# Strassen's scheme of seven products in the first matmul of both feed-forward parts of an encoder trunk

## What is computed

```python
FF = 2816; D_MODEL = 1024
def swiglu(xn, w_in, w_out):
    gu = xn @ w_in                  # w_in: (1024, 5632), gate columns, then up columns
    g = gu[..., :FF]
    u = gu[..., FF:]
    return (jax.nn.silu(g) * u) @ w_out   # w_out: (2816, 1024)

xn = rmsnorm(h, norm_ffn[i]); h = h + swiglu(xn, ffn_w_in[i], ffn_w_out[i])
```

## Time and profile before

| | |
|---|---|
| runs of the kernel before | 2137.39 us median of 3 (2136.59 to 2147.86) |
| span of the profiled execution | 2135.1 us |
| PE, weight loads | 2074.0 us (97%), 1865.6 us (87%) |
| DVE, ACT, POOL | 840.1, 448.3, 722.5 us (39%, 21%, 34%) |
| matmuls | 11553 |
| DMA | 110.93 MB, mean 52 GB/s |

### The profile page before, as it was taken

The page is one execution under the profiler, slowest core; times in us unless marked ns, Lnnn a source line. Parts: engine busy times, 40 slices in busy tenths (PEclk is TensorE's granted clock), DMA queues, the critical chain, the costliest instruction groups (busy, mean ns, idle before and its releaser), DMA issues.

```text
span 2135.1 us, 30482 instructions
## 1 busy us (share of the span) xinstructions
PE 2074.0 (97%) x11553; PEld 1865.6 (87%) x11553; DVE 840.1 (39%) x1458; ACT 448.3 (21%) x895; POOL 722.5 (34%) x423
## 2 busy tenths in 40 slices
PE   7999999999999999999999999999899999999999
PEld 7787878899999999999978777787788888888887
DVE  6544354543221222124655555556442212221231
ACT  4222322322100010001233333334221100100001
POOL 3221312234443444444411111111244444443443
PEclk9999999999999999999999999999899999999999
DMA  3111111122222222221211111010122222222222
GB/s 115 40 30 30 49 30 40 30 72 60 66 61 59 59 59 60 59 63 53 71 30 30 30 30 29 20 29 20 40 60 59 69 59 66 62 62 67 59 59 89
DMA packets 213393, 110.93 MB, mean 52 GB/s; under 512 B 5283, under 2 KB 212294, under 8 KB 213334
## 3 DMA queue, kind: packets, MB, share of 16 engines
q1 hardware_dynamic: 209264, 108.28, 17.4%
q10 hardware_dynamic: 4070, 1.81, 0.3%
HBM read 106.93 MB, written 3.15 MB: 52 GB/s over the span
## 4 chain that ended last, share of the span: by engine, by line
PE 92%; DVE 4%; issue 2%; ACT 1%; DMA 0%; DVEq 0%; ACTq 0%; SPq 0%
PE ps L412 77%; PE ps L584 4%; PE ps L704 3%; PE ps L682 2%; PE ps L568 1%; PE ps L694 1%; PE ps L634 1%; DVE rstd L820 1%; PE ps L593 0%; PE ps L521 0%; PE ps L651 0%; DVE wk L1126 0%; PE ps L669 0%; DVE mx L1107 0%; PE ps L553 0%
## 5 line engine op out<-in xcount | busy, mean ns | idle before, releaser
L381 POOL CAST wh<-raw 128x1024 fp32r<-128x1024 f32 x200 | 208.6, 1043 | 1378.2 <-PE ps L412 1370.7
L412 PE MATMUL ps<-xh,wh 128*128 128x400 f32 (+2 forms) x2176 | 583.5, 348 | 9.1 <-DVE wk L788 4.0
L412 PE MATMUL ps<-xl,wh 128*128 128x400 f32 (+2 forms) x2176 | 570.9, 342 | 0.0
L412 PE MATMUL ps<-xh,wl 128*128 128x400 f32 (+2 forms) x2176 | 568.6, 342 | 0.0
L383 POOL TENSOR_TENSOR wl<-raw,wh 128x1024 fp32r<-128x1024 f32 x200 | 509.1, 2545 | 16.0
L412 PEld LDWEIGHTS ps<-xh,wh 128*128 128x128 f32 x2176 | 370.9, 189 | 44.5 <-issue 20.3
L412 PEld LDWEIGHTS ps<-xl,wh 128*128 128x128 f32 x2176 | 377.9, 189 | 17.1
L412 PEld LDWEIGHTS ps<-xh,wl 128*128 128x128 f32 x2176 | 375.6, 189 | 17.5
L412 PE MATMUL ps<-yh,wh 128*128 128x400 f32 (+1 forms) x960 | 252.7, 344 | 3.5 <-DVE yl L1141 3.5
L412 PE MATMUL ps<-yl,wh 128*128 128x400 f32 (+1 forms) x960 | 250.7, 342 | 0.0
L412 PE MATMUL ps<-yh,wl 128*128 128x400 f32 (+1 forms) x960 | 250.6, 342 | 0.0
(11 more groups left out here) (169 smaller groups left out, 1609.8 us busy)
## 6 DMA issues: line engine op xcount, KB each, us to landing
raw<-in_ffn_w_in_dram SPq DMA_DIRECT2D x88, 512.0 KB, 3.8
raw<-in_ffn_w_out_dram SPq DMA_DIRECT2D x32, 512.0 KB, 3.8
raw<-in_d_w_in_dram SPq DMA_DIRECT2D x24, 512.0 KB, 3.8
raw<-in_m_w_in_dram SPq DMA_DIRECT2D x22, 512.0 KB, 3.8
raw<-in_ffn_w_out_dram SPq DMA_DIRECT2D x16, 384.0 KB, 3.3
raw<-in_m_w_out_dram SPq DMA_DIRECT2D x8, 512.0 KB, 3.8
raw<-in_d_w_out_dram SPq DMA_DIRECT2D x8, 512.0 KB, 3.8
wk<-in_x_prompt_dram SPq DMA_DIRECT2D x4, 512.0 KB, 5.6
```

The source lines that it names most:

```text
L381: pool.tensor_copy(wh[:, slot, :], raw[:, slot, :]).then_inc(w_hi, 1)
L412: mm = pe.matmul(out, w[:, slot, k * P:(k + 1) * P], x[:, k, a:b], start=(k + q == 0), stop=(k == k_tiles - 1 and q == 2), skip_group_chec ...
```

## The change

The first product of both layers is a product of a 2 x 2 block matrix: rows are the gate block and the up block of one pair, the inner dimension is the even and the odd k-tiles (4 each), columns are the first and the second half of the tokens (400 + 400 in layer 0, 384 + 384 in layer 1). Instead of eight sub-products it makes seven, in Winograd's form of Strassen's scheme. For each pair:

- Seven products of 4 k-tiles, three matmuls each: 84 matmuls of 400 (384) columns where there were 96 (with 800 or 768 columns for two). They go to three PSUM banks, and pairs take turns with two sets of three. Some products are added onto an earlier one in its bank, after ACT has copied what stood there: product 3 waits for the copy of product 1, product 5 for that of product 3 (`copy_ready`), and product 7 until DVE has read its bank (`sum_ready`).
- The weights come as four quarters of 256 KB (gate/up x even/odd k-tiles). DVE makes four sums of quarters in place (`sum_1` to `sum_4`, 128 x 512 each). ACT makes the seven high parts (128 x 512), POOL the seven low parts (128 x 512). Before, POOL made both, for two blocks of 128 x 1024.
- The results: ACT copies three (128 x 400), DVE adds or scales four out of PSUM, then scales the gate row (128 x 800) and half of the up row, multiplies, and makes `fyl`.
- The token side is made once per layer: the output product of the mixer no longer makes `xh` and `xl` but, per pair of blocks, four combinations of token halves (`combinations`), seven high parts on ACT and seven low parts on DVE, 14 pieces per two blocks into `sx`.
- `GROUPS` becomes 6, 6, 6, 4, as SBUF is laid out anew by hand (`place`). The loops of the feed-forward parts are unrolled.
- In the second product PE runs blocks 0 and 1 up to their last k-tile, then the last k-tile of both. The setup of the rotary tables moves to the end of layer 0's feed-forward part.

```diff
-GROUPS = (8, 8, 6)
+GROUPS = (6, 6, 6, 4)
+NPROD = 7
+B11, T1, T2, B21, T3, B22, T4 = range(NPROD)
+BANK_OF = (BANK_R, BANK_Q, BANK_R, BANK_Z, BANK_R, BANK_Q, BANK_R)
```

SyncE, for each pair g after a group's first, loads the four quarters:

```diff
+                        load_quad(1, 1, g, layer)
+                        sp.wait_ge(wsum_ready, 4 * g)
+                        sp.wait_ge(prod_split, NPROD * (g - 1) + 3)
+                        load_quad(0, 0, g, layer)
+                        sp.wait_ge(prod_split, NPROD * (g - 1) + 5)
+                        load_quad(1, 0, g, layer)
+                        sp.wait_ge(prod_split, NPROD * (g - 1) + 6)
+                        load_quad(0, 1, g, layer)
```

GpSimd makes the low part of each of the seven weight combinations:

```diff
+            def split_product(g, j):
+                pool.wait_ge(prod_hi, NPROD * g + j + 1)
+                pool.tensor_tensor(slot_of(j, 1), factor(g, j), slot_of(j, 0).bitcast(F32),
+                                   ALU.subtract).then_inc(prod_split, 1)
```

TensorE, one pair, and the start of a second product:

```diff
+            def pair_products(g, layer, n0, first):
+                if g >= 2:
+                    pe.wait_ge(sum_ready, 4 * (g - 1))
+                if g == first:
+                    pe.wait_ge(acc_free, n0 - 1 + XT)
+                product(g, 0, layer)
+                product(g, 1, layer)
+                pe.wait_ge(copy_ready, 3 * g + 1)
+                product(g, 2, layer)
+                if g == first:
+                    pe.wait_ge(acc_free, n0 + XT)
+                product(g, 3, layer)
+                if g == layer * FT:
+                    sum_squares(2 * layer + 2)
+                pe.wait_ge(copy_ready, 3 * g + 3)
+                product(g, 4, layer)
+                product(g, 5, layer)
+                pe.wait_ge(sum_ready, 4 * g + 2)
+                product(g, 6, layer)
...
+                    pe.wait_ge(yl_ready, y - 1)
+                    run_block(n0, 0, 0, ys, tiles, tokens=tokens, k1=tiles - 1)
+                    run_block(n0 + 1, 1, banks[1], ys, tiles, tokens=tokens, k1=tiles - 1)
+                    pe.wait_ge(yl_ready, y)
+                    run_block(n0, 0, 0, ys, tiles, tokens=tokens, k0=tiles - 1)
+                    run_block(n0 + 1, 1, banks[1], ys, tiles, tokens=tokens, k0=tiles - 1)
```

VectorE, pair g of a group (`finish` takes the last result of the pair before, multiplies, and makes `fyl`):

```diff
+                        if i:
+                            finish(g - 1, i - 1)
+                        if more:
+                            sum_1(g + 1)
+                            sum_2(g + 1)
+                            sum_3(g + 1)
...
+                        ve.tensor_tensor(gt[:, first_half], product_bank(g, 3, layer), p1[:, 0:w],
+                                         ALU.add).then_inc(sum_ready, 1)
...
+                        ve.tensor_tensor(ut[:, second_half], product_bank(g, 4, layer), p5[:, 0:w],
+                                         ALU.add).then_inc(sum_ready, 1)
+                        if more:
+                            sum_4(g + 1)
...
+                        ve.tensor_tensor(gt[:, second_half], product_bank(g, 5, layer), u2[:, 0:w],
+                                         ALU.add).then_inc(sum_ready, 1)
+                        if g == f0:
+                            invert(2 * layer + 2)
+                        ve.wait_ge(sum_ready, 4 * g + 3)
+                        ve.tensor_tensor(gt[:, 0:2 * w], gt[:, 0:2 * w], rstd[:, 0:2 * w], ALU.mult).then_inc(g_ready, 1)
```

ScalarE, pair g, and behind the last pair of a group the high parts for the next one:

```diff
+                        copy(g, 0, p1, 1)
+                        if more:
+                            weight_high(g + 1, 0, n0, first)
+                        if i:
+                            y_high(g - 1, i - 1)
...
+                        copy(g, 1, p5, 2)
+                        if more:
+                            weight_high(g + 1, 1, n0, first)
+                        copy(g, 2, u2, 3)
+                        if more:
+                            weight_high(g + 1, 2, n0, first)
+                            weight_high(g + 1, 3, n0, first)
...
+                            weight_high(g + 1, 4, n0, first)
+                            weight_high(g + 1, 5, n0, first)
+                        sc.wait_ge(g_ready, g + 1)
+                        sc.activation(gt[:, 0:2 * w], gt[:, 0:2 * w], ACT.Silu).then_inc(silu_ready, 1)
+                        if more:
+                            weight_high(g + 1, 6, n0, first)
+                    y_high(first + tiles - 1, tiles - 1)
+                    if gi < len(GROUPS) - 1:
+                        for j in range(NPROD):
+                            weight_high(first + tiles, j, n0 + KT, first + tiles)
```

More of the change, by code:

```diff
@@ L61 @@
 FFN0 = OUT0 + KT
-NFF = 2 * FT + KT * len(GROUPS)
+NFF = KT * len(GROUPS)
 MIX1 = FFN0 + NFF
@@ L74, with pair_groups @@
 ATTN_SET = 8
+NPROD = 7
+B11, T1, T2, B21, T3, B22, T4 = range(NPROD)
+BANK_R, BANK_Q, BANK_Z = range(3)
+BANK_OF = (BANK_R, BANK_Q, BANK_R, BANK_Z, BANK_R, BANK_Q, BANK_R)
+OPENS = (0, 1, 3)
+WIDTH = (HT, TQ // 2)
+def pair_groups(layer):
+    first = layer * FT
+    for gi, tiles in enumerate(GROUPS):
+        yield gi, first, tiles, (FFN0, FFN1)[layer] + KT * gi
+        first += tiles
 SWAP = [i ^ (ROPE_DIM // 2) if i < ROPE_DIM else i for i in range(32)]
@@ L426, in sum_squares @@
                 for out, a, b in parts:
-                    mm = pe.matmul(out, ones[:, :], wk[:, 6, a:b], start=True, stop=True)
+                    mm = pe.matmul(out, ones[:, :], src[:, a:b], start=True, stop=True)
                 mm.then_inc(norm_sum, 1)
@@ new lines, in combinations, with low @@
+            def combinations(layer, k):
+                n0, w, g = (OUT0, OUT1)[layer], WIDTH[layer], layer * FT
+                first, second = slice(0, w), slice(w, 2 * w)
+                done = KP * NPROD * layer + NPROD * k
+                sums = 4 * (KP * layer + k)
+                norm = 2 * layer + 1
+                def low(j, src):
+                    ve.wait_ge(sxh_ready, done + j + 1)
+                    ve.tensor_tensor(sx[layer][:, k * NPROD + j, 1, :], src,
+                                     sx[layer][:, k * NPROD + j, 0, :].bitcast(F32), ALU.subtract).then_inc(sxl_ready, 1)
+                add_block(n0, 2 * k, 3 if layer and k == 0 else 0)
+                ve.wait_ge(xf_ready, KT * layer + 2 * k + 1)
+                ve.tensor_tensor(tx1[:, 0:w], xe[:, second], xe[:, first], ALU.subtract).then_inc(tx_ready, 1)
+                low(B11, xe[:, first])
+                add_square(2 * k + KT * norm)
+                low(T1, tx1[:, 0:w])
+                if k == KP - 1:
+                    sum_1(g)
+                    sum_2(g)
+                add_block(n0, 2 * k + 1, 1)
+                ve.wait_ge(xf_ready, KT * layer + 2 * k + 2)
+                ve.wait_ge(tx_ready, sums + 1)
+                ve.tensor_tensor(tx2[:, 0:w], xo[:, second], tx1[:, 0:w], ALU.subtract).then_inc(tx_ready, 1)
+                ve.tensor_tensor(xe[:, second], xo[:, second], xe[:, second], ALU.subtract).then_inc(tx_ready, 1)
+                low(T2, tx2[:, 0:w])
+                low(B21, xo[:, first])
+                ve.wait_ge(tx_ready, sums + 2)
+                ve.tensor_tensor(xo[:, first], xo[:, first], tx2[:, 0:w], ALU.subtract).then_inc(tx_ready, 1)
+                if k == KP - 1:
+                    sum_3(g)
+                low(T3, xe[:, second])
+                low(B22, xo[:, second])
+                low(T4, xo[:, first])
+                add_square(2 * k + 1 + KT * norm)
+                if k == KP - 1:
+                    sum_4(g)
@@ L1206, in _ @@
             deliver(D_HEADS - 1, 1)
-            out_blocks(OUT1, 3, FFNN + KT)
-            ffn(FFN1, 1)
+            for k in range(KP):
+                combinations(1, k)
+            ffn(1)
         @block.scalar
```

523 lines of the change are left out of this document (344 added, 179 removed).

## The result

| | before | changed |
|---|---|---|
| median | 2137.77 us (2136.59 to 2151.66, 5 runs) | 2171.15 us (2159.51 to 2173.45, 5 runs) |
| ratio, 95% interval | 1 | 1.0117 [1.008, 1.0154] |
| profiled run: time, span | 2137.4, 2135.1 | 2159.5, 2157.7 |
| matmul instructions | 11553 | 11025 |
| PE's mean granted clock | 0.987 | 0.969 |

The change makes the kernel slower by 1.2%, where -5.5 us, 2131.9, was forecast. In a later comparison on one chip, the changed kernel took 2167.06 us (2161.92 to 2172.39) against 2147.49 (2137.39 to 2152.26, 12 runs): 1.0093 [1.0062, 1.0124]. The program before has times between 2137 and 2152 us, and they go with the clock that it is granted: 2137.6 at 0.987, 2148.9 at 0.982, 2151.5 at 0.981. A median of a few such runs can lie anywhere between, so what follows is read from profiles, by stage.

The account below looks back on a forecast made before the run. PE, busy 97% of the span, was taken as the bound. -93.5 saved + 12 + 24 + 22 + 17 + 3 + 10 = -5.5 us gave 2131.9 against 2137.4 us; range 2100 to 2180.

Parts of the forecast that it names:

- The saving: First products of both layers: 264 fewer matmuls per layer, each worth its full cadence on PE, -93.5 us.
- The loop of a pair: Steady pairs: loop taken as 15.5 us in layer 0 and 15.35 in layer 1, +12 us (0 to 35).
- the sum of demands: Layer 0 pair: POOL 9.1 and DVE 6.3 us as one resource, less overlap at changes of hands, 14.3 us.
- The turns: Within a pair: DVE's SBUF work and POOL's subtractions exclude each other, overlapping about 0.13 us at each change of hands.
- Start of a layer: First pairs of both layers: PE waits 10.0 us for ACT's copy, then 2.6 a pair later, +24 us (18 to 30).
- Start of a second product: Before block 2: PE waits 2.8 us for POOL's weight split, in eight groups, +22 us (20 to 24).
- Start of a later group: First pair of six later groups: PE waits 2.9 us for ACT's copy behind seven high parts, +17 us (14 to 22).
- Layer 0's last group: 4-tile blocks shorter than DVE's and ACT's 5.3 us per block, +3 us (0 to 8); rotary setup there costs nothing.
- The clock in the feed-forward parts: Falls to 1.2 GHz after both 10 us waits and about 4 in 10 of 16 shorter ones, +10 us (3 to 32).
- The third rival: Clock falls after each of the 18 waits, 32 us instead of 10: 2154 us, chance 0.08.
- The first rival: Waits at their short ends, 64 us in all with the clock: 2108 us, chance 0.30.
- the second (DVE and POOL hold PE): Every pair: no overlap at changes of hands, loop 16.3 to 16.4 us, 32 us more: 2164 us, chance 0.22.

Follow-up runs that it names:

- f1_slack: The changed kernel with each pair's low part computed twice on DVE, in pairs followed by another of their group: 2182.96 us, 1.0183 against the kernel before.
- e3_groups: The changed kernel with layer 0's groups of pairs in the order 4, 6, 6, 6: 2146.04 us, 1.0019 against the kernel before.
- e5_all: e4 with layer 0's groups as 4, 6, 6, 6 and the rotary setup behind block 1: 2112.56 us, 0.9813 against the kernel before.
- b_order: The kernel before with only block 1's two pieces in the second product cut as the change cuts them: 2156.5 us, 1.0047 against the kernel before.
- e1: The changed kernel with ACT's copy of product 1 ahead of the high parts that wait for the fourth sum: 2168.73 us, 1.0099 against the kernel before.
- e4: e2_blocks with ACT's three first-pair copies ahead of the next pair's high parts, root and reciprocal one step earlier: 2132.41 us, 0.9923 against the kernel before.
- e6: e5_all with DVE making a group's first pair's own two sums ahead of the next pair's three: 2110.48 us, 0.9845 against the kernel before.
- e2_blocks: The changed kernel with block 1 of a second product cut behind its first tile instead of before its last: 2144.77 us, 0.9995 against the kernel before.

## Why the prediction was wrong

Forecast -5.5 us, measured +22.6 in the profiled spans, 28 us apart. Two steps failed above all: the clock was taken to fall behind 4 in 10 of the shorter waits, where it fell behind 12 of 16, and the refill behind a wait was put at nothing. The length of the waits together was nearly right. By the prediction's own terms:

- **The saving**, -93.5: right. The steady stretches keep the cadence of 180 and 172 ns.
- **The loop of a pair**, +12: 1.0. It was taken as 15.5 and 15.35 us and is at most about 14.2 and 14.5. The mistake is the step that walked the chain with POOL's subtractions and DVE's sums all behind one another and then added handovers; the sum of demands, 14.3 us, was in the same text and is close to what f1_slack gives. The turns themselves are as told: at 632.71 DVE started 0.08 us into POOL's 1.27 us and ended 0.56 after it, so 0.12 of its 0.68 overlapped. One reading of the earlier trace rows was loose: the instruction with an operand in PSUM wasn't inside POOL's 2.35 us but ended 0.39 after it; it does show 0.99 us without a delay.
  The Trainium skill (SBUF — State Buffer, "Who interferes with whom") has the other engine fully blocked; the overlap is small, and it isn't what decided.
- **Start of a layer**, +24: 8.63 + 2.02 + 8.96 + 2.19 = 21.8, less 0.5. Right, 3 too much.
- **Start of a second product**, +22: seven of 2.62 to 2.68, 18.6. Right in place and size. The eighth belongs to layer 0's last group.
- **Start of a later group**, +17: 2.83, 2.83, 2.85, 3.02, 3.02, 3.02, 17.6. Right.
- **Layer 0's last group**, +3: 5.07 + 0.34 + 1.28 + 0.61 + 1.27 + 4.57 = 13.1, of which 2.8 were counted above. The step that failed is "so it costs nothing". The setup did end as block 2's weights were ready (1011.96 and 1011.76), even with 1.8 us lost to POOL in its turn at `lam`; but a memset and the add of block 0, which frees the bank, stand behind it and end at 1014.12. In the other two profiles of the program the setup lost two and three turns, and the wait was 6.11 and 8.47. The 4.57 us at the end, where the next part waits for the last block's low part, were not looked for at all; e3_groups and e5_all remove them.
- **Refill behind a wait**, not priced: 0.26 us each in b_order, and 25 new waits of over 0.25 us give 6.5. What is left in the stages once saving, idle time and clock are taken off is 13.5 + 93.5 - 71.5 - 24.1 = 11.4, so some 5 us stay without a name.
- **The clock in the feed-forward parts**, +10: 24.1. It fell behind 12 of the 16 shorter waits, where 4 in 10 were taken; the price of a fall, 1.7 us, was right. The rows used, 3.75 us idle in 50 that cost nothing, consist of gaps of at most 1.2 us each, and say nothing of one of 2 or 3. The third rival, a fall behind each wait (2154), was the nearest in kind to what happened and had a chance of 0.08.
  What the Trainium skill (TensorE: Matmul & The Clock Gate, "HAM oscillation — how this bites in real kernels") says of waits in a loop that bring the clock down each time, the trace bears out in kind, for 15 of 19 waits, though these don't come round in one loop.
- **Attention**, not looked at, +10: unchanged code with the same idle time. The second profile of before shows 13 us of difference between two executions, so this term belongs to the kernel only in part; the feed-forward parts make +13.5 without it. 1.7 us of the 10 follow the wait of 4.57 us at the stage's first matmul.

In sum: idle time came 6.5 us lower than forecast, 71.5 against 78, and refill with what has no name (11.4), more clock (14.1) and attention (10.0) made 35.5; the mixer ahead of them was 0.9 shorter. That the idle time came so near is partly luck: the loop was 11 us too high and layer 0's last group 10 too low.

The first rival (short ends) put the idle time at 60.5 us, further off than the forecast, the second (DVE and POOL hold PE) is refuted by the steady stretches and by f1_slack. The direction was wrong because a wait was sized as little more than its length. With 1.4 to 2.1 us of clock behind most of the waits over 2 us and 0.26 of refill, one of 2.6 us costs 4.3 to 5.0 where the clock falls and 2.9 where it doesn't.

## What to carry to other kernels

An algebraic saving on a full PE is worth its whole cadence only while each operand is early, and the losses sit where a steady run begins and ends: price every head, tail and change of stage before the loop. Price a wait of PE above 2 us at its length plus 0.3 us plus, in three cases of four here, 1.7 us of clock. An engine's queue that holds both what PE wants now and what it wants next must be read to its end: freeing the first late operand (e1, e4, e6) only showed the second. And an edit that moves one engine's work can move it onto another's turn, as e2_blocks did with the rotary setup.
